# Other tile order, other matmul shapes and overlapped units in the attention of a one-core decoder step

## The reference, cut to what matters

```python
s = einsum('bkgqd,bknd->bkgqn', qi, k_cmp) - slopes * d_c          # compressed blocks
p_c = where(ok_c, softmax(where(ok_c, s, NEG_INF)), 0.0)
o_c = einsum('bkgqn,bknd->bkgqd', p_c, v_cmp)
...
p_s = softmax(where(d_s >= 0, s, NEG_INF)); o_s = einsum(p_s, vg)  # selected blocks
p_w = softmax(where(ok_w, s, NEG_INF));     o_w = einsum(p_w, vw)  # sliding window
return gi[..., 0:1] * o_c + gi[..., 1:2] * o_s + gi[..., 2:3] * o_w
```

## Time and profile before

| | |
|---|---|
| median of three runs | 2756.91 us |
| profiled execution | 2758.13 us, its span 2756.5 us |
| PE busy | 2542.9 us (92%) |
| DVE, ACT, POOL busy | 1731.6 (63%), 1138.2 (41%), 378.7 us (14%) |
| mean granted TensorE clock | 0.962 of 2.4 GHz |
| DMA | 78 GB/s over the span |

### The profile page before, as it was taken

The page is one execution under the profiler, slowest core; times in us unless marked ns, Lnnn a source line. Parts: engine busy times, 40 slices in busy tenths (PEclk is TensorE's granted clock), DMA queues, the critical chain, the costliest instruction groups (busy, mean ns, idle before and its releaser), DMA issues.

```text
span 2756.5 us, 59359 instructions
## 1 busy us (share of the span) xinstructions
PE 2542.9 (92%) x24673; PEld 2333.0 (85%) x24673; DVE 1731.6 (63%) x3000; ACT 1138.2 (41%) x2194; POOL 378.7 (14%) x396
## 2 busy tenths in 40 slices
PE   5999989997888899999989979999998898899997
PEld 5999987675877668999987879999975568899997
DVE  6687865576544347787861167779735434777796
ACT  5354430332222105454530364545427743545453
POOL 3000000000222411000013030000028741100000
PEclk9999999998999799999999989999989997999999
DMA  5322321110000022222346312223311011222232
GB/s 197 104 84 92 115 87 47 39 64 37 3 4 3 5 77 92 92 85 95 111 130 147 125 63 92 85 87 110 126 58 43 9 47 46 77 89 79 93 113 73
DMA packets 46074, 215.45 MB, mean 78 GB/s; under 512 B 6256, under 2 KB 6384, under 8 KB 30096
## 3 DMA queue, kind: packets, MB, share of 16 engines
q1 hardware_dynamic: 37152, 174.34, 19.3%
q0 software_dynamic: 8720, 38.28, 4.7%
HBM read 202.49 MB, written 12.17 MB: 78 GB/s over the span
## 4 chain that ended last, share of the span: by engine, by line
PE 53%; DVE 6%; POOL 4%; ACT 3%; issue 3%; DMA 0%; POOLq 0%; DVEq 0%; ACTq 0%; SPq 0%
PE banks L744 22%; PE banks L705 16%; PE banks L907 2%; PE banks L879 2%; POOL arena L3073 2%; PE banks L895 1%; DVE ring_l L2239 1%; PE banks L1550 1%; PE banks L1492 1%; PE banks L1420 1%; PE banks L1526 1%; ACT arena L2046 1%; PE banks L1476 1%; PE banks L761 1%; PE banks L1393 1%
## 5 line engine op out<-in xcount | busy, mean ns | idle before, releaser
L744 PE MATMUL banks<-xop_h,ring_h 128*128 128x272 f32 x2296 | 662.9, 289 | 18.7 <-ACT banks L1831 7.9
L744 PE MATMUL banks<-xop_l,ring_h 128*128 128x272 f32 x2296 | 661.0, 288 | 0.0
L744 PE MATMUL banks<-xop_h,ring_l 128*128 128x272 f32 x2296 | 660.0, 287 | 0.0
L744 PEld LDWEIGHTS banks<-xop_h,ring_h 128*128 128x128 f32 x2296 | 433.3, 189 | 22.7 <-DVE ring_l L2239 5.2
L744 PEld LDWEIGHTS banks<-xop_h,ring_l 128*128 128x128 f32 x2296 | 433.1, 189 | 0.0
L744 PEld LDWEIGHTS banks<-xop_l,ring_h 128*128 128x128 f32 x2296 | 432.2, 188 | 0.0
L705 PE MATMUL banks<-hh,wh 128*128 128x272 f32 x1408 | 292.0, 289 | 1.1 <-DVE arena L2417 1.1
L705 PE MATMUL banks<-hl,wh 128*128 128x272 f32 x1408 | 291.1, 288 | 0.0
L705 PE MATMUL banks<-hh,wl 128*128 128x272 f32 x1408 | 289.0, 286 | 0.0
L1672 ACT ACTIVATE ring_h<-arena 128x512 fp32r<-128x512 f32 x328 | 205.8, 627 | 156.6 <-PE banks L744 56.5
L2239 DVE TENSOR_TENSOR ring_l<-arena,ring_h 128x512 fp32r<-128x512 f32 x328 | 225.0, 686 | 3.7 <-ACT ring_h L1672 2.5
(11 more groups left out here) (381 smaller groups left out, 4465.4 us busy)
## 6 DMA issues: line engine op xcount, KB each, us to landing
raw<-in_w_in SPq DMA_DIRECT2D x88, 1024.0 KB, 4.9
raw<-in_w_out SPq DMA_DIRECT2D x96, 384.0 KB, 3.1
raw<-in_w_out SPq DMA_DIRECT2D x32, 256.0 KB, 2.7
raw<-in_w_rk SPq DMA_DIRECT2D x8, 1024.0 KB, 4.8
arena<-in_pages_c POOLq DMA_DIRECT2D x32, 256.0 KB, 7.2
raw<-in_w_kv SPq DMA_DIRECT2D x6, 1024.0 KB, 5.5
raw<-in_w_v SPq DMA_DIRECT2D x4, 1024.0 KB, 5.1
raw<-in_w_o SPq DMA_DIRECT2D x4, 1024.0 KB, 4.9
```

Of the source, the lines that this page charges most:

```text
L744: ins = mm(pst[:, bank, 0:HALF], wt[:, w], x, start=first, stop=last, skip_group_check=True)
```

## The change

- The order of query tiles in a head pair is 3, 0, 2, 1 (`ROUND_TILES`), on all engines.
- In a round, both score groups and the compressed one come first, then the first half of the transposes, `values(S-3)`, the second half.
- Compressed values and probabilities are padded by zeros to 128 rows. POOL clears `vcmp_p` after the eighth compression piece, ahead of the store of keys and values; and `ptc`'s upper half ahead of the window loads.
- The page loads go from POOL to SP, the load of the window values to the front of POOL's attention part.
- POOL's multiplication has a second factor of 1.0.
- `sample_scores` takes the two samples of a unit in turn for each piece of keys, one on each half of the columns. `sample_values` has the probabilities stationary (32 columns, four quarters in turn) and values moving (128 columns); results are row by feature, in bank 4 or 5; ACT copies them out (`sample_rows`), PE transposes them into bank 0.
- Two units are under way at a time: scores of units 0 and 1 in rounds 32 and 33, of units 2 and 3 behind the transposes of 0 and 1; ACT and DVE in a matching order.
- Four semaphores become one that counts POOL's clearings.

```diff
+ROUND_TILES = (3, 0, 2, 1)
+
+
 def turns_to(S):
 
-    return sum(3 if x % 4 < 2 else 5 for x in range(S))
+    return sum(3 if ROUND_TILES[x % 4] < 2 else 5 for x in range(S))
...
-        vcmp_p, vcmp_d = ar(TAIL + 320, 256, p1=64), ar(TAIL + 576, 256)
+        vcmp_p, vcmp_d = ar(TAIL + 320, 256), ar(TAIL + 576, 256)
...
-        ptc = ar(VSLC_C + 4096, 2, P, p1=64)
+        ptc = ar(VSLC_C + 4096, 2, P)
...
+            sp.wait_ge(table_in, 16)
+            sp.wait_ge(gate_mm, 1)
+            for n in range(DEC_B * NPG):
+                page = sp.value_load(ptab[0:1, n:n + 1], min_val=0, max_val=I["pages"].shape[0] - 1)
+                sp.dma_start(kslc_c[:, n:n + 1].rearrange("p o x t -> p (o x t)"),
+                             I["pages"][bass.ds(page, 1), :, 0:256].rearrange("o p c -> p (o c)"))\
+                    .then_inc(pages_in, 16)
+                sp.dma_start(vslc_c[:, n:n + 1, :].rearrange("p o c -> p (o c)"),
+                             I["pages"][bass.ds(page, 1), :, 256:512].rearrange("o p c -> p (o c)"))\
+                    .then_inc(pages_in, 16)
             stream_split("bo", I["w_bo"], free=lambda: sp.wait_ge(turned, turns_to(PAIRS - 2)))
...
                 out = [pst[64 * p:64 * p + 64, 5, qt * P:(qt + 1) * P] for p in range(2)]
-                mm(out[0], vcmp_p[0:32, c[0]], ptc[0:32, S % 2, :], start=True, stop=False, skip_group_check=True)
+                if S == 0:
+                    pe.wait_ge(pool_cleared, PTC_CLEAR)
                 for n, v in enumerate((v_slc, v_win)):
                     for x in range(qt + 1):
-                        for p in (1, 0):
+                        for p in range(2):
                             mm(out[p], v[:, x, c[p]], pt[p][:, 512 * n + P * x:512 * n + P * x + P],
-                               start=(p == 1 and n == 0 and x == 0), stop=(p == 0 and n == 1 and x == qt),
-                               skip_group_check=True)
-                mm(out[1], vcmp_p[32:64, c[1]], ptc[32:64, S % 2, :], start=False, stop=True, skip_group_check=True)\
-                    .then_inc(o_mm, 1)
+                               start=(n == 0 and x == 0), stop=False, skip_group_check=True)
+                for p in range(2):
+                    last = mm(out[p], vcmp_p[:, c[p]], ptc[:, S % 2, :], start=False, stop=True,
+                              skip_group_check=True)
+                last.then_inc(o_mm, 1)
...
-                for j in range(2):
-                    b = 2 * u + j
-                    r = slice(64 * j, 64 * j + 64)
-                    for out, src in ((pst[r, bank, 0:128], lambda x: kcmp[:, x, 32:160]),
-                                     (pst[r, bank, 128:160], lambda x: kslc[:, x, SEQ:TOK]),
-                                     (pst[r, bank, 160:192], lambda x: kwin[:, x, SEQ:TOK]),
-                                     (pst[r, bank + 1, 0:256].rearrange("p (g t) -> p g t", g=NPG),
-                                      lambda x: kslc_c[:, 2 * b:2 * b + 2, x, :]),
-                                     (pst[r, bank + 1, 256:512], lambda x: kwin_c[:, b, x, :])):
-                        for x in range(2):
-                            last = mm(out, qbd[:, x, b, :], src(x), start=(x == 0), stop=(x == 1))
+                for cols, src in ((slice(0, 128), lambda b, x: kcmp[:, x, 32:160]),
+                                  (slice(128, 160), lambda b, x: kslc[:, x, SEQ:TOK]),
+                                  (slice(160, 192), lambda b, x: kwin[:, x, SEQ:TOK]),
+                                  (slice(512, 768), lambda b, x: kslc_c[:, 2 * b:2 * b + 2, x, :]),
+                                  (slice(768, 1024), lambda b, x: kwin_c[:, b, x, :])):
+                    c0 = cols.start % 512
+                    for x in range(2):
+                        for j in range(2):
+                            out = pst[64 * j:64 * j + 64, bank + cols.start // 512, c0:c0 + cols.stop - cols.start]
+                            if cols.start == 512:
+                                out = out.rearrange("p (g t) -> p g t", g=NPG)
+                            last = mm(out, qbd[:, x, 2 * u + j, :], src(2 * u + j, x), start=(x == 0), stop=(x == 1),
...
+                elif u == 1:
+                    pe.wait_ge(o_taken, DT)
+                else:
+                    pe.wait_ge(o_rows, u - 1)
                 pt = ptb[u % 2]
-                for x in range(2):
-                    c = slice(x * P, (x + 1) * P)
-
-                    def both(ap, x=x):
-                        return ap.rearrange("p (j x r) -> p x j r", j=2, x=2)[:, x]
-
-                    out = pst[:, 4, P * u:P * (u + 1)]
-                    mm(both(out), vcmp_d[:, c], both(pt[:, 0, :]), start=True, stop=False, skip_group_check=True)
+                terms = [(0, lambda b, c: vcmp_d[:, c])]
+                for pg in range(NPG):
+                    terms += [(1 + pg, lambda b, c, pg=pg: vslc_c[:, 2 * b + pg, c]),
+                              (3 + pg, lambda b, c, pg=pg: vwin_c[:, 2 * b + pg, c])]
+                terms += [(5, lambda b, c: v_new[:, 0, c]), (6, lambda b, c: v_new[:, 1, c])]
+                for n, (block, v) in enumerate(terms):
+                    k = P if block < 5 else 32
                     for j in range(2):
-                        b, rows = 2 * u + j, slice(64 * j + 32 * x, 64 * j + 32 * x + 32)
-                        for pg in range(NPG):
-                            mm(out[:, rows], vslc_c[:, 2 * b + pg, c], pt[:, 1 + pg, rows],
-                               start=False, stop=False, skip_group_check=True)
-                            mm(out[:, rows], vwin_c[:, 2 * b + pg, c], pt[:, 3 + pg, rows],
-                               start=False, stop=False, skip_group_check=True)
-                    mm(both(out), v_new[:, 0, c], both(pt[0:32, 5, :]), start=False, stop=False,
-                       skip_group_check=True)
-                    last = mm(both(out), v_new[:, 1, c], both(pt[0:32, 6, :]), start=False, stop=True,
-                              skip_group_check=True)
+                        for x in range(2):
+                            rows = slice(64 * j + 32 * x, 64 * j + 32 * x + 32)
+                            last = mm(pst[rows, 4 + u % 2, 0:P], pt[0:k, block, rows],
+                                      v(2 * u + j, slice(x * P, (x + 1) * P)), start=(n == 0),
+                                      stop=(n == len(terms) - 1), skip_group_check=True)
                 last.then_inc(o_mm, 1)
 
             for S in range(PAIRS + 3):
                 live = S < PAIRS
+                turning = 2 <= S < PAIRS + 2
                 if live:
                     scores(S, 0)
+                    scores(S, 1)
+                    scores_cmp(S)
+                if turning:
+                    turn_probs(S - 2, 0)
                 if S >= 3:
                     values(S - 3)
-                if live:
-                    scores(S, 1)
-                    scores_cmp(S)
-                if S == PAIRS:
-                    sample_scores(0)
-                if 2 <= S < PAIRS + 2:
-                    turn_probs(S - 2, 0)
+                if PAIRS <= S < PAIRS + 2:
+                    sample_scores(S - PAIRS)
+                if turning:
                     turn_probs(S - 2, 1)
                     turn_cmp(S - 2)
             for u in range(4):
                 sample_turns(u)
-                if u < 3:
-                    sample_scores(u + 1)
+                if u < 2:
+                    sample_scores(u + 2)
                 sample_values(u)
+            for u in range(4):
+                pe.wait_ge(o_rows, u + 1)
+                last = pe.transpose(pst[:, 0, P * u:P * (u + 1)], sample_buf[u][:, 704:832], ident)
+            last.then_inc(turned, 1)
...
+            act.wait_ge(pool_cleared, VCMP_CLEAR)
...
+            def sample_rows(u):
+                act.wait_ge(o_mm, PAIRS + u + 1)
+                act.activation(sample_buf[u][:, 704:832], pst[:, 4 + u % 2, 0:P], ACT.Copy).then_inc(o_rows, 1)
+
+            for S in range(PAIRS + 2):
+                if S == PAIRS + 1:
+                    sample_exps(0)
+                if S >= 2:
+                    copies(S - 2)
+                if S < PAIRS:
+                    exps(S)
+            sample_exps(1)
+            for u in range(4):
+                sample_copies(u)
+                if u >= 1:
+                    sample_rows(u - 1)
+                if u < 2:
+                    sample_exps(u + 2)
+            sample_rows(3)
...
+            sample_maxes(0)
+            sample_maxes(1)
+            dve.wait_ge(gates_d_in, 16 * DEC_B)
+            for u in range(4):
+                sample_factors(u)
                 if u == 0:
                     take_out(DT - 1)
-            dve.wait_ge(o_mm, PAIRS + 4)
+                if u < 2:
+                    sample_maxes(u + 2)
+            dve.wait_ge(turned, turns_to(PAIRS) + 9)
...
```

(23 more changed lines are left out.)

65 lines of the change are left out of this document (33 added, 32 removed).

## The result

The changed kernel takes 2713.3 us (median of 4 runs, 2711.02 to 2716.05) where the kernel before, beside it, takes 2757.6. The ratio is 0.9836, with a 95% interval of 0.9819 to 0.9853. It is 1.6% faster, 44 us; the forecast was 2724, 34 us.

The account below looks back on a forecast made before the run. Prompt: no engine full, PE, ACT and POOL near it, so hand-over order counts; samples: PE. Gains 16 + 22 less 4 make 34 us; 2758.1 - 34 - 1.2 = 2723, said 2724, own range 2712 to 2732, overall 2710 to 2760.

Parts of the forecast that it names:

- Prompt, 16 us: Prompt attention: with cheap POOL scaling, a four-round period of 21.2 us instead of 23.79, 16 us gained.
- This alone is worth nothing.: Prompt rounds: moving page loads from POOL to SP gains nothing alone, since POOL kept up in the old order.
- Compressed pair, at least 0.3 us a round: Prompt values: a 128-row pair replacing 32-row matmuls takes at least 0.3 us per round off PE, 32 times.
- Tile order: Prompt, order 3, 0, 2, 1: no work changes, first transposes start later, 3 us more before round 4.
- Clock: Prompt's part: the forecast is wrong if the granted clock there leaves 2.4 GHz.
- POOL's factor: POOL's scaling in the prompt: a second multiplication by 1.0 brings its price to 0.6 to 0.75 of the present.
- Samples, 22 us: Samples' attention: 76.2 us become 54, between 46 at full clock and 62 at half; 22 us gained.
- Store, 4 us: Store of keys and values, queued behind the eighth compression piece: lands later, 2.7 to 5.1 us lost, 4 taken.
- POOL's price unchanged: Rival on POOL's scaling: the second multiplication changes no price, prompt gains 0, 2739 to 2740 us; chance 0.24.
- POOL dearer: Rival on POOL's scaling: the operation costs more, 2765 us at 1.3 times, about 2790 at 1.6; chance 0.15.
- No packing: Rival on the samples' matmuls: column parts don't run side by side, 20 us back, 2744 us; chance 0.10.
- all at full clock: Rival: samples at full clock take 46 us and POOL is cheap, 8 us more come off, 2715 us; chance 0.08.

Follow-up runs that it names:

- e3: Changed kernel with the prompt's values back between the two score groups of a round: 2713.8 us, ratio 0.984.
- e1: Changed kernel with POOL's scaling back in its one-multiplication form: 2733.2 us, ratio 0.9915.
- e2: Kernel before with one edit, POOL's scaling in its two-multiplication form: 2756.6 us, ratio 0.9995.
- e10: Changed kernel with the compressed values again as one 32-row matmul ahead of the 128-row ones and one behind: 2713.2 us, ratio 0.985.
- e4: Changed kernel with the query tiles in the order 0, 1, 2, 3: 2720.6 us, ratio 0.9868.
- e9: Changed kernel with tiles in the order 0, 1, 2, 3 and values between the two score groups: 2726.9 us, ratio 0.9907.
- e8: Changed kernel with DVE taking unit u+1's factors and scaling ahead of unit u+2's maxima in the samples' part: 2704.5 us, ratio 0.9816.
- e5: Changed kernel with the samples' scores issued for one column half after the other: 2715.7 us, ratio 0.9859.
- e6: Changed kernel with the samples' values issued for one column quarter after the other: 2721.9 us, ratio 0.9876.

## Why the prediction was right

The direction, the two big terms and the mechanism of each held; the sizes were all off in the same direction, and the result lies at the lower end of the forecast's own 2712 to 2732. What the forecast had not was the clock in the prompt's part.

*Prompt, 16 us.* Measured on the forecast's own marks, 181.8 became 161.1 (2048.29 to 2209.42): 20.7 us. (The mark of before, 2224.64, is the first score group of round 31 and not the last; both kernels are measured to the start of that round.) The period came to 20.36, not 21.2. The mis-sized term is ACT's waiting: 2.7 us in place of 3.4. Of PE's waits the 1.9 us ahead of compressed turns are of five turns, one of them of the round before; four have 1.5. Both score groups in a row were to save 0.2 us a round and saved 0.17 (e3). The forecast rightly said that everything hangs on POOL's being cheap (e1: 22 us). That its price within the interval hardly matters no run shows: only 0.447 and 1 were measured.
*"This alone is worth nothing."* Said of the page loads that leave POOL; the loads weren't tried alone. What e2 shows is that making POOL twice as fast was worth 0.8 us in the old order. The other load, the gates, which stayed on POOL, did cost 2.3 to 3.2 us in the new order, and the forecast had not priced it.
*Compressed pair, at least 0.3 us a round.* Measured 0.48 in PE's work; on the path 0.29 over the stretch of e10 and 0.20 in its late periods.
*Tile order.* "No work changes" is true, but I gave it no gain of its own, only a slower start. It is worth 12 to 14 us, some 8 of them because the long waits are gone behind which the clock fell.
*Clock.* The forecast called itself wrong if the granted clock in the prompt's part left 2.4 GHz. It did, for 3.41 us behind the wait for the gates, in the first profile of the changed kernel and not in the second; that cost some 0.8 us and upset nothing. In the orders of e4 and e9 the same thing costs 8 us.
*POOL's factor.* Taken at 0.6 to 0.75, measured 0.447: the side was right, from the cheaper two-operand row, and the size was missed. The forecast's estimate of 0.7 us for 512 columns, from the limit of 1.03 cycles per element in the Trainium skill, GPSIMD Engine Reference, "Performance versus the Vector engine", was the better one; the trace agrees with 0.70. It doesn't hold for the one-multiplication form, still 1.57 us in e1.
*Samples, 22 us.* On the forecast's marks 76.2 became 47.5 (2209.42 to the result's copies at 2256.96): 28.7. I took 54 between 46 at full clock and 62 at half; only the part from 2246.8 on ran at half. Scores took 2.85 us. The forecast's 2.5 was a slip: 2816 columns at its own rate of 1024 in 1.09 us are 3.0 (and its 3.5 us for values at that rate are 3.8). Values took 1.87 (2.3 forecast), steps between units 7.8, 7.8 and 5.2 (7.9, 7.9, 4.4). The bound named, DVE's maxima ahead of factors, is what e8 confirms.
*Store, 4 us.* Found in the place named, with DVE waiting for it, at 1.76 us. The mis-sized term is the landing: 9.4 us where 10 to 12.3 were reckoned.
*Rivals.* POOL's price unchanged would have been 2733.2 (e1), for 2740 forecast. POOL dearer did not occur. No packing is refuted by e5 and e6. The number that came out, 2713, is that of the rival "all at full clock" (2715), but not for its reason: the last 15 us of the stretch were at 1.2 GHz. The three terms came out 4.7, 6.7 and 2.2 us better than forecast, and that execution lost 5.5 in stages without an edit.

## What to carry to other kernels

An engine that is far from full can still decide an order: the same edit on POOL was worth 0.8 us in one order and 22 in the other, so price it in the order in which it will run. Where two or four column parts of an array work on the same rows, alternate them instruction by instruction. After a gain, read the new waits one by one: here five of them, each a matter of what stands first in an engine's queue or of whose queue it stands in, gave another 14 us. And look at the granted clock before giving a loss to an order: more than half of what the old tile order costs here is clock.

## What the hardware did that I had not expected

- GpSimd's tensor_scalar with one multiplication takes 2.52 ns a column, with a second (by 1.0) 0.82, on 128 partitions in fp32. The fixed part is 0.28 us in both.
- Four column quarters overlap nearly fully: 56 instructions in 1.87 us, 33 ns each, and 127 ns each in sequence.
- Inside the prompt part the granted clock fell to 1.2 GHz, for 3.41 us at a time (6.8 in one case), behind single waits of PE of 1.58 to 2.31 us, in 15 of 23 cases, and behind none of up to 1.12 us. Each such fall cost 1.6 us in e4's and e9's periods. What decides between the cases stays open.
